# Eight sums over partitions moved from TensorE to GpSimd in a one-core decoder layer

## Chip, cores and metric

The kernel runs on one core of one Trainium2 chip. The metric is the device time of one execution in microseconds, lower is better.

## What is computed

One layer of a decoder trunk, 256 tokens of width 2048, all in float32:

```python
mod = silu(c) @ w_ada + b_ada                 # 6 x 2048: sh1, sc1, gt1, sh2, sc2, gt2
h = rmsnorm(x, g_pre_mix) * (1 + sc1) + sh1
y = token_mixer(h)                            # 4 GLA heads, 8 attention heads, merged by two sigmoid gates
x = x + gt1 * rmsnorm(y, g_post_mix)
h = rmsnorm(x, g_pre_ffn) * (1 + sc2) + sh2
y = conv_ffn(h)                               # up to 2 x 5632, causal conv of width 3, gelu gate, down
out = x + gt2 * rmsnorm(y, g_post_ffn)
```

In the mixer, one input projection gives the GLA and attention operands and the two gates; each branch is projected to 2048, `merged = sigmoid(gate_a) * y_a + sigmoid(gate_b) * y_b`, and a projection `w_o` follows.

## The kernel before

**Weights.** Every weight passes through four buffers `raw`, `hi`, `lo` of 128x2048 (fill number `w`, buffer `w % 4`). SyncE loads fill `w` into `raw` in two transfers once TensorE has finished fill `w - 4` (semaphore `used`). ScalarE rounds it to `hi` (`split_hi`), VectorE makes the remainder `lo = raw - hi` (`split_lo`, L761), and TensorE multiplies activations, themselves split in two, by `hi` and by `lo` (`tokens_still`, `weights_still`, `one_row_tile`; all their products have line L1246). ScalarE and VectorE work three fills ahead (`split_lo(w + 3)`).

**Stages**, one after the other on TensorE: the gate stage (32 fills, and one for the low-rank factor), four heads of 12 fills (`HEAD_N`; tile `n` of head `I`), the merge stage (`MERGE`: 16 fills `m`, four column blocks `cb` of 512 with two branches and two halves each), the output projection with `w_o` (16 fills `kt`), the up projection (22 passes of four fills) and the down projection (44 fills). Every engine's order is written out by hand as loops over these numbers; nothing is scheduled at run time.

**In a head**, VectorE makes per tile the decay operands `Mb` of a level and selects into `A` (L924 to L934), for which TensorE's `gram` products wait, in tile 9 the softmax, and in the last tile of head 3 the first two remainders of the branch outputs `og_om` (`branch_lo`, L960), which the merge stage needs.

**In the merge stage**, VectorE multiplies and adds a block's two branches (`merged(cb)`, L1030 to L1033, at m = 5, 7, 11, 15), TensorE transposes the result (`merged_T`, L1475, one tile later), and VectorE makes its remainder (`merged_lo`, L1038).

**Modulation.** `silu(c) @ w_ada` is made without TensorE's weights: a *unit* is one row block of `w_ada`, 128 partitions x 1024 columns, which VectorE scales by a column of `silu(c)` and adds to an accumulator. Sixteen units make a *part*, 1024 columns of `mod` as 128 partial sums. The parts of `sh1` and `sc1` belong to the gate stage and are left alone by the change. The other eight (0 to 3: `sh2` and `sc2`; 4, 5: `gt1`; 6, 7: `gt2`) alternate between `acc_a` and `acc_b`, from part 6 on in `acc_a` alone. GpSimd issues their transfers (L440) into two buffers `ada`, each when the unit before last has been used (`ada_used`), and behind them on the same queue the bias rows (L415) and the post-norm gains G1 and G2 (L428, L435). VectorE's `ada_unit` stands behind the split, `UNITS_H[n]` times in a head's tile, `UNITS_L[n]` in the last head's, `UNITS_M[m]` in the merge stage's; in the up projection `row_unit` (L1170) does two per pass.

**The sums over the 128 partitions** are TensorE's. For parts 0 to 3, at tile 5 of head 0 to 3, eight products with the accumulator as weights and a column of ones give the part as columns, which VectorE copies into `mods` (L1017). For parts 4 to 7, `row_sums` multiplies the accumulator by an all-ones matrix: two products of 128x512, four records, whose every row is the sum; VectorE multiplies them into the gain (`gate_row`, L1062). Two stand in the output projection (kt = 0 and 2), one each in passes 8 and 17 of the up projection. `zero_acc` clears an accumulator for parts 4 to 7, and a bias row is loaded into it.

## Time and profile before

| | us |
|---|---|
| median of 3 runs | 1479.89 |
| lowest, highest | 1479.24, 1482.47 |
| the profiled execution's own time | 1481.32 |
| its span, first to last instruction | 1479.5 |
| TensorE busy in it | 1444.7 |
| VectorE busy in it | 1103.2 |
| mean granted clock of TensorE | 0.997 |

In the profile PE is TensorE's matmul, PEld its weight load, DVE is VectorE, ACT ScalarE, POOL GpSimd, SP SyncE. Times are from the span's start. A timeline row gives start, duration, engine, line, operation, output and inputs, shape and count, and in brackets the engine's idle time ahead of it and what ended that. Durations of pipelined matmuls are modelled, so their spacing is read from the starts.

### The profile page before, as it was taken

What the parts mean: (1) busy time and instruction counts of PE and PEld (TensorE: products, weight loads), DVE (VectorE), ACT (ScalarE), POOL (GpSimd) and SP (SyncE); (2) the same over time, 40 slices, a digit from 0 to 9 for tenths busy, and PEclk for the clock granted to TensorE, in tenths of its full rate; (3) what the DMA queues carried; (4) which work ended last, traced back from release to release, by engine and by line L of the source; (5) the groups of instructions that cost most, each with busy time, mean ns of one, the idle gap of its engine ahead of it and who ended that gap; (6) DMA issues with size and microseconds to landing.
All of it is one profiled execution on the core that took longest, in us unless ns stands there. A gap on an engine that the chain in (4) does not pass through costs nothing.

```text
span 1479.5 us, 19948 instructions
## 1 busy us (share of the span) xinstructions
PE 1444.7 (98%) x7444; PEld 1230.8 (83%) x7444; DVE 1103.2 (75%) x1129; ACT 701.6 (47%) x711; POOL 86.5 (6%) x177
## 2 busy tenths in 40 slices
PE   4999999999999999999999999999999999999998
PEld 2878888888888888878888888888888888888886
DVE  6999988898888988855687877777776666555445
ACT  4454444354535465424565455545544545434443
POOL 3000001111111000100000000000000000000000
PEclk9999999999999999999999999999999999999999
DMA  9999879898979877866467777677765555555553
GB/s 362 386 387 379 292 252 323 263 296 272 313 245 317 266 243 260 303 239 218 163 223 235 239 231 237 202 224 238 242 228 182 187 194 188 189 195 198 191 190 129
DMA packets 235816, 367.07 MB, mean 248 GB/s; under 512 B 11487, under 2 KB 161505, under 8 KB 234994
## 3 DMA queue, kind: packets, MB, share of 16 engines
q1 hardware_dynamic: 215824, 294.69, 59.5%
q0 software_dynamic: 18848, 69.23, 13.6%
q10 hardware_dynamic: 1090, 2.40, 0.4%
q8 instruction: 37, 0.61, 0.2%
q14 instruction: 17, 0.14, 0.0%
HBM read 364.18 MB, written 2.10 MB: 248 GB/s over the span
## 4 chain that ended last, share of the span: by engine, by line
PE 86%; DMA 6%; DVE 5%; ACT 1%; issue 1%; SPq 0%; DVEq 0%
PE ps L1246 85%; DMA ada<-in_w_ada 4%; DMA raw<-in_w_in 1%; DVE acc_a L790 1%; DVE acc L771 1%; DMA adar<-in_w_ada 1%; DVE lo L761 1%; ACT hi L454 1%; DMA raw<-in_w_o 0%; ACT yt L672 0%; PE ps L1475 0%; DVE acc_b L790 0%; SPq L312 0%; DVE yo L1094 0%; PE ps L1406 0%
## 5 line engine op out<-in xcount | busy, mean ns | idle before, releaser
L1246 PE MATMUL ps<-hT,hi 128*128 128x512 f32 x1936 | 466.0, 393 | 0.9 <-DVE hT L1116 0.9
L1246 PEld LDWEIGHTS ps<-hT,hi 128*128 128x128 f32 x1936 | 356.2, 188 | 72.3 <-issue 2.0
L454 ACT ACTIVATE hi<-raw 128x2048 fp32r<-128x2048 f32 x116 | 222.1, 1916 | 280.6 <-DMA raw<-in_w_in 185.5
L761 DVE TENSOR_TENSOR lo<-raw,hi 128x2048 fp32r<-128x2048 f32 x117 | 266.9, 2285 | 63.1 <-ACT hi L454 62.9
L1246 PEld LDWEIGHTS ps<-hT,lo 128*128 128x128 f32 x1936 | 248.2, 191 | 9.4
L1246 PE MATMUL ps<-hT,lo 128*128 128x256 f32 x1936 | 251.1, 283 | 0.0
L1201 DVE TENSOR_TENSOR lo<-raw,hi 128x2048 fp32r<-128x2048 f32 x88 | 199.1, 2290 | 32.6 <-ACT hi L719 32.4
L1246 PE MATMUL ps<-hi,hT 128*128 128x512 f32 x768 | 185.4, 394 | 1.1 <-DVE hT L815 0.9
L1246 PE MATMUL ps<-hi,asp 128*128 128x512 f32 x704 | 175.9, 389 | 0.0
L719 ACT ACTIVATE hi<-raw 128x2048 fp32r<-128x2048 f32 x88 | 165.6, 1906 | 11.2 <-DMA raw<-in_w_up 9.3
L1246 PEld LDWEIGHTS ps<-hi,hT 128*128 128x128 f32 x768 | 143.1, 189 | 32.5 <-issue 2.9
L1246 PEld LDWEIGHTS ps<-hi,asp 128*128 128x128 f32 x704 | 132.1, 188 | 27.5
L1225 DVE TENSOR_TENSOR lo<-raw,hi 128x2048 fp32r<-128x2048 f32 x40 | 91.7, 2292 | 49.5 <-ACT hi L732 49.5
L440 POOL DMA_DIRECT2D ada<-in_w_ada x128 | 68.1, 532 | 879.4 <-DVE acc_a L1170 295.2
L1246 PE MATMUL ps<-lo,asp 128*128 128x512 f32 x352 | 96.1, 389 | 0.0
L1246 PE MATMUL ps<-lo,hT 128*128 128x512 f32 x384 | 94.8, 389 | 0.0
L697 ACT ACTIVATE cv<-ps 128x512 f32<-128x512 f32 x44 | 26.4, 600 | 134.3 <-PE ps L1246 134.3
L771 DVE SCALAR_TENSOR_TENSOR acc<-adar,scol,acc 128x1024 f32<-128x1024 f32 x60 | 77.0, 1284 | 10.8 <-DMA adar<-in_w_ada 6.7
L1246 PEld LDWEIGHTS ps<-lo,hT 128*128 128x128 f32 x384 | 72.1, 188 | 15.0
L1246 PEld LDWEIGHTS ps<-lo,asp 128*128 128x128 f32 x352 | 66.0, 188 | 13.8 <-DVE lo L761 0.2
L708 ACT ACTIVATE asp<-aT 128x256 fp32r (+1 forms) x44 | 18.0, 416 | 124.7 <-PE ps L1246 124.7
L732 ACT ACTIVATE hi<-raw 128x2048 fp32r<-128x2048 f32 x40 | 76.0, 1901 | 0.0
(207 smaller groups left out, 1269.6 us busy)
## 6 DMA issues: line engine op xcount, KB each, us to landing
raw<-in_w_up SPq DMA_DIRECT2D x176, 512.0 KB, 4.4
raw<-in_w_in SPq DMA_DIRECT2D x162, 512.0 KB, 5.7
ada<-in_w_ada POOLq DMA_DIRECT2D x128, 512.0 KB, 4.9
raw<-in_w_down SPq DMA_DIRECT2D x88, 512.0 KB, 4.2
adar<-in_w_ada SPq DMA_DIRECT2D x64, 512.0 KB, 10.3
raw<-in_w_o SPq DMA_DIRECT2D x32, 512.0 KB, 5.1
raw<-in_w_gla_out SPq DMA_DIRECT2D x16, 512.0 KB, 5.1
raw<-in_w_moba_out SPq DMA_DIRECT2D x16, 512.0 KB, 5.3
```

What stands on the lines that cost most here:

```text
L440: pool.dma_start(ada[:, u % 2, :], wada[:, t, PART_COL[part]:PART_COL[part] + 1024]).then_inc(ada_in[u % 2], 16)
L454: act.activation(hi[:, w % 4, :], raw[:, w % 4, :], ACT.Copy).then_inc(hi_done, 1)
L697: act.activation(cv[:, :, :], ps[:, 2 * g:2 * g + 2, TOK:], ACT.Copy).then_inc(cross5, 1)
L708: act.activation(asp[:, k, 0:TOK], aT[:, ds(kt, 1), :], ACT.Copy).then_inc(a_hi, 1)
L719: act.activation(hi[:, w % 4, :], raw[:, w % 4, :], ACT.Copy).then_inc(hi_done, 1)
L732: act.activation(hi[:, (w + 3) % 4, :], raw[:, (w + 3) % 4, :], ACT.Copy).then_inc(hi_done, 1)
L761: dve.tensor_tensor(lo[:, w % 4, :], raw[:, w % 4, :], hi[:, w % 4, :].bitcast(F32), ALU.subtract).then_inc(lo_done, 1)
L771: ins = dve.scalar_tensor_tensor(a, adar[:, u % 8, :], scol[:, t:t + 1], a, ALU.mult, ALU.add)
L790: ins = dve.scalar_tensor_tensor(acc[:, :], ada[:, u % 2, :], scol[:, t:t + 1], acc[:, :], ALU.mult, ALU.add)
L1201: dve.tensor_tensor(lo[:, k, :], raw[:, k, :], hi[:, k, :].bitcast(F32), ALU.subtract).then_inc(lo_done, 1)
L1225: dve.tensor_tensor(lo[:, k, :], raw[:, k, :], hi[:, k, :].bitcast(F32), ALU.subtract).then_inc(lo_done, 1)
L1246: return pe.matmul(out_, lhsT, rhs, start=start, stop=stop)
```

## The change

All eight sums are made by GpSimd: `partition_all_reduce` over the accumulator, in place, every partition gets the sum. It stands on GpSimd's queue ahead of the third unit transfer of the next part, and one on a single column is made ahead of all. For parts 0 to 3 a row goes to DRAM (`part_rows`) and comes back as columns three units later; `acc_zero` and the first unit of parts 2 and 3 wait for that. `gate_row` reads the accumulator itself. G1 is loaded at unit 68 instead of 90, and x in the merge stage (behind fill 8) instead of the output projection. The units are dealt out anew: 54 in the heads instead of 67 (with the gate stage's 12 as before), 19 in the merge stage instead of 17, 11 in the output projection instead of none; where a tile has two, one stands ahead of the split. TensorE's queue has lost its sums, in the output projection the transposes of block 3 stand behind the third half tile, and in the up projection each sum's gate row moves from pass 8 to 9 and 17 to 19.

```diff
@@ -73,10 +73,13 @@
     UNITS_3 = {25: 1, 26: 1, 27: 1, 28: 2, 29: 2, 30: 2, 31: 2, 32: 1}
-    UNITS_H = [2, 1, 1, 1, 1, 1, 1, 2, 2, 2, 2, 2]
-    UNITS_L = [2, 1, 1, 1, 1, 1, 1, 2, 2, 1, 0, 0]
-    UNITS_M = [1] * 13 + [2] + [1] * 2
-    assert sum(UNITS_3.values()) + (HEADS - 1) * sum(UNITS_H) + sum(UNITS_L) + sum(UNITS_M) == 6 * KT
+    UNITS_H = [[1, 1, 1, 1, 1, 1, 0, 1, 2, 1, 2, 1],
+               [1, 1, 1, 2, 1, 1, 1, 1, 0, 1, 2, 1],
+               [1, 1, 1, 2, 1, 2, 1, 1, 1, 1, 0, 1],
+               [1, 1, 2, 1, 2, 1, 2, 1, 1, 1, 1, 1]]
+    UNITS_M = [0, 1, 2, 1, 2, 1, 2, 2, 2, 1, 1, 1, 0, 1, 2, 0]
+    UNITS_O = [1] * 11 + [0] * 2
+    assert sum(UNITS_3.values()) + sum(sum(h) for h in UNITS_H) + sum(UNITS_M) + sum(UNITS_O) == 6 * KT
...
@@ -336,13 +341,13 @@
                 load_grid(W_MERGE + m, wmo if branch else wgo, 4 * half, 4, 512 * cb, 512)
+                if m == 8:
+                    sp.wait_ge(oo_ready, 4)
+                    sp.dma_start(x2[:, :, :], x_v).then_inc(xr_in, 16)
             for kt in range(KT):
                 sp.wait_ge(used, W_WO + kt - 3)
                 load_row(W_WO + kt, wo, kt)
-                if kt == 4:
-                    sp.wait_ge(oo_ready, 4)
-                    sp.dma_start(x2[:, :, :], x_v).then_inc(xr_in, 16)
             def load_up(i, w, n):
...
@@ -415,14 +420,33 @@
                 pool.dma_start(acc[0:1, :], b_ada[:, PART_COL[part]:PART_COL[part] + 1024]).then_inc(bias_in, 16)
+            def sum_rows(part, acc):
+                pool.wait_ge(ada_used, KT * part + KT)
+                pool.partition_all_reduce(acc[:, :], acc[:, :], P, bass.bass_isa.ReduceOp.add).then_inc(row_sum, 1)
+                if part < 4:
+                    pool.wait_ge(row_sum, part + 1)
+                    pool.dma_start(part_rows[part:part + 1, :], acc[0:1, :]).then_inc(row_out, 16)
+
+            def row_columns(part):
+                pool.wait_ge(row_out, 16 * (part + 1))
+                pool.dma_start(modsf[:, M_SH2 * KT + 8 * part:M_SH2 * KT + 8 * part + 8],
+                               part_rows[part].rearrange("(k p) -> p k", p=P), allow_slow_non_contiguous=True).then_inc(part_in, 16)
+
+            made(pool.memset(stat[:, 9:10], 0.0))
+            made(pool.partition_all_reduce(stat[:, 9:10], stat[:, 9:10], P, bass.bass_isa.ReduceOp.add))
+
             pool.wait_ge(mod_done, 4)
             for u in range(8 * KT):
                 part, t = divmod(u, KT)
+                if t == 2 and part:
+                    sum_rows(part - 1, acc_b if part in (2, 4, 6) else acc_a)
+                if t == 5 and 0 < part < 5:
+                    row_columns(part - 1)
                 if u == 4 * KT - 2:
                     bias_row(4, acc_a)
                 if u == 5 * KT - 2:
                     bias_row(5, acc_b)
-                if u == 6 * KT - 6:
+                if u == 4 * KT + 4:
                     pool.wait_ge(pv_done, HEADS)
...
@@ -438,6 +462,7 @@
                 pool.dma_start(ada[:, u % 2, :], wada[:, t, PART_COL[part]:PART_COL[part] + 1024]).then_inc(ada_in[u % 2], 16)
+            sum_rows(7, acc_a)
         @block.scalar
...
@@ -791,6 +816,10 @@
             def zero_acc(part):
+                if part < 6:
+                    dve.wait_ge(part_in, 16 * (part - 1))
+                else:
+                    dve.wait_ge(g_ready, part - 5 if part == 6 else 3)
                 dve.memset((acc_b if part == 5 else acc_a)[:, :], 0.0).then_inc(acc_zero, 1)
...
@@ -1012,15 +1041,12 @@
                         tail(I - 1, n)
-                    if n == 6:
-                        dve.wait_ge(mod_done, 4 + I + 1)
-                        dve.tensor_copy(modsf[:, M_SH2 * KT + 8 * I:M_SH2 * KT + 8 * I + 8], ps[:, 6, 0:8]).then_inc(part_read, 1)
-                    if (I, n) == (2, 8):
+                    if (I, n) == (3, 4):
                         zero_acc(4)
-                    if (I, n) == (3, 7):
-                        zero_acc(5)
+                    if UNITS_H[I][n] > 1:
+                        ada_unit()
                     split_lo(w + 3)
-                    for k in range(UNITS_H[n] if I < HEADS - 1 else UNITS_L[n]):
+                    if UNITS_H[I][n]:
                         ada_unit()
...
@@ -1050,31 +1076,39 @@
                     merged({5: 0, 7: 1, 11: 2, 15: 3}[m])
+                if m == 6:
+                    zero_acc(5)
+                if UNITS_M[m] > 1:
+                    ada_unit()
                 split_lo(w + 3)
-                for k in range(UNITS_M[m]):
+                if UNITS_M[m]:
                     ada_unit()
-            assert ada_count[0] == 6 * KT
-
-            def gate_row(k, G, bank, sem_in):
+
+            def gate_row(k, G, acc, sem_in):
                 cs = slice(1024 * (k % 2), 1024 * (k % 2 + 1))
-                dve.wait_ge(g_done, k + 1)
+                dve.wait_ge(row_sum, 4 + k + 1)
                 dve.wait_ge(sem_in, 16)
-                dve.tensor_tensor(G[:, cs], ps[:, bank:bank + 2, :].rearrange("p b n -> p (b n)"), G[:, cs], ALU.mult).then_inc(g_ready, 1)
+                dve.tensor_tensor(G[:, cs], acc[:, :], G[:, cs], ALU.mult).then_inc(g_ready, 1)
             for kt in range(KT - 3):
-                if kt == 0:
-                    gate_row(0, G1, 4, g1_in)
                 split_lo(W_WO + kt + 3)
                 if kt == 0:
                     merged_lo(3)
-                    gate_row(1, G1, 4, g1_in)
-                if kt == 2:
+                if UNITS_O[kt]:
+                    ada_unit()
+                if kt == 3:
+                    gate_row(0, G1, acc_a, g1_in)
+                if kt == 4:
                     zero_acc(6)
-                if kt == 4:
+                if kt == 8:
+                    dve.wait_ge(part_in, 64)
                     link(dve.tensor_tensor(mods[:, M_SH2:M_GT2, :], mods[:, M_SH2:M_GT2, :],
                                            cols[:, M_SH2 * KT:5 * KT].rearrange("p (m k) -> p m k", m=2), ALU.add))
                     dve.scalar_tensor_tensor(mods[:, M_SC2, :], mods[:, M_SC2, :], 1.0, cols[:, COL_PRE2:COL_PRE2 + KT],
                                              ALU.add, ALU.mult).then_inc(mods_ready, 1)
+
+            assert ada_count[0] == 6 * KT
+            gate_row(1, G1, acc_b, g1_in)
             def y_sum(branch, tt):
...
@@ -1202,18 +1236,20 @@
                     if sums is not None and n == 2:
-                        gate_row(sums - 4, G2, 4 if sums == 6 else 6, g2_in)
+                        gate_row(sums - 4, G2, acc_a, g2_in)
                         if sums == 6:
                             zero_acc(7)
             up_pass(0, row=(6, 0), tasks=(2, 3))
             with dve.Fori(1, 8) as i:
                 up_pass(i, row=(6, 0))
-            up_pass(8, sums=6)
-            with dve.Fori(9, 17) as i:
-                up_pass(i, row=(7, 9))
-            up_pass(17, sums=7)
-            with dve.Fori(18, UP_ITERS - 1) as i:
+            up_pass(8)
+            up_pass(9, sums=6)
+            with dve.Fori(10, 18) as i:
+                up_pass(i, row=(7, 10))
+            up_pass(18)
+            up_pass(19, sums=7)
+            with dve.Fori(20, UP_ITERS - 1) as i:
                 up_pass(i)
...
@@ -1443,17 +1479,10 @@
                         gram(I, n - 3)
-                    if n == 5:
+                    if n == 9:
+                        pe.wait_ge(evac, 5 * I + 4)
                         if I:
                             pe.wait_ge(om_f, I)
-                        pe.wait_ge(ada_used, KT * I + KT)
-                        acc = acc_b if I % 2 else acc_a
-                        for j in range(8):
-                            ins = mm(ps[:, 6, j:j + 1], acc[:, P * j:P * (j + 1)], ones[:, 0:1])
-                        ins.then_inc(mod_done, 1)
-                    if n == 9:
-                        pe.wait_ge(evac, 5 * I + 4)
-                        pe.wait_ge(part_read, I + 1)
                         for hd in range(2):
...
@@ -1516,22 +1540,15 @@
                     one_row_tile(k, mT[:, kt, :], kt == 0, False, 0, W_WO + kt + 1)
-                if kt == 0:
-                    pe.wait_ge(ada_used, 5 * KT)
+                if kt == 2:
+                    merged_T(3)
                     pe.wait_ge(gated_y, 7)
-                    row_sums(acc_a, 4)
-                if kt == 1:
-                    merged_T(3)
-                if kt == 2:
-                    pe.wait_ge(ada_used, 6 * KT)
-                    pe.wait_ge(g_ready, 1)
-                    row_sums(acc_b, 4)
+                    one_row_tile(W_WO % 4, mT[:, 0, :], True, False, 1, W_WO + 1, (0, 1))
+                    one_row_tile((W_WO + 1) % 4, mT[:, 1, :], False, False, 1, W_WO + 2, (0, 1))
                     pe.wait_ge(mt_ready, 4)
-                    one_row_tile(W_WO % 4, mT[:, 0, :], True, False, 1, W_WO + 1, (2, 3))
-                    pe.wait_ge(g_ready, 2)
-                    one_row_tile(W_WO % 4, mT[:, 0, :], True, False, 1, W_WO + 1, (0, 1)).then_inc(used, 1)
-                    for j in (1, 2):
-                        one_row_tile((W_WO + j) % 4, mT[:, j, :], False, False, 1, W_WO + j + 1).then_inc(used, 1)
+                    one_row_tile(W_WO % 4, mT[:, 0, :], True, False, 1, W_WO + 1, (2, 3)).then_inc(used, 1)
+                    one_row_tile((W_WO + 1) % 4, mT[:, 1, :], False, False, 1, W_WO + 2, (2, 3)).then_inc(used, 1)
+                    one_row_tile((W_WO + 2) % 4, mT[:, 2, :], False, False, 1, W_WO + 3).then_inc(used, 1)
                 if 3 <= kt < KT - 4:
...
@@ -1572,18 +1589,9 @@
                                   None if order == range(4) else h2_is_ready).then_inc(used, 1)
-                    if sums is not None and n == 1:
-                        pe.wait_ge(ada_used, KT * sums + KT)
-                        row_sums(acc_a, 4 if sums == 6 else 6)
             up_pass(0, order=UP_FIRST)
-            with pe.Fori(1, 8) as i:
-                up_pass(i)
-            up_pass(8, 6)
-            with pe.Fori(9, 17) as i:
-                up_pass(i)
-            up_pass(17, 7)
-            with pe.Fori(18, UP_ITERS) as i:
+            with pe.Fori(1, UP_ITERS) as i:
                 up_pass(i)
```

The places the prediction speaks of follow as the instructions stand on an engine.

GpSimd, end of part 4 (`G_113` is G1, `acc_a` holds part 4, `acc_b` parts 3 and 5). Before, from unit 62 on:

```order
L415 DMA acc_a<-in_b_ada 1x16x64
L440 DMA ada<-in_w_ada 128x1024 x16
L415 DMA acc_b<-in_b_ada 1x16x64
L440 DMA ada<-in_w_ada 128x1024 x12
L428 DMA G_113<-in_g_post_mix 128x2048
```

Now:

```order
L420 DMA acc_a<-in_b_ada 1x16x64
L464 DMA ada<-in_w_ada 128x1024 x4
L425 ISA acc_b<-acc_b 128x1024
L428 DMA part_rows<-acc_b 16x1x64
L464 DMA ada<-in_w_ada 128x1024 x2
L452 DMA G_113<-in_g_post_mix 128x2048
L464 DMA ada<-in_w_ada 128x1024
L432 DMA mods<-part_rows 128x8x1
L464 DMA ada<-in_w_ada 128x1024 x9
```

The sum (`ISA`) and the row's transfer stand between two unit transfers, the gain's load two units behind them.

VectorE, merge stage, from block 0's sum at m = 5 to block 1's at m = 7 (`lo<-raw,hi` is a split, `acc` with `ada` a unit, `GA` the block). Before:

```order
L1033 TENSOR_TENSOR GA<-GA 128x2x512
L761 TENSOR_TENSOR lo<-raw,hi 128x2048
L790 SCALAR_TENSOR_TENSOR acc_b<-ada,scol,acc_b 128x1024
L761 TENSOR_TENSOR lo<-raw,hi 128x2048
L790 SCALAR_TENSOR_TENSOR acc_b<-ada,scol,acc_b 128x1024
L1038 TENSOR_TENSOR mT<-ps,mT 128x4x256
L1030 TENSOR_TENSOR GA<-GA,ps 128x2x512
```

Now:

```order
L1059 TENSOR_TENSOR GA<-GA 128x2x512
L786 TENSOR_TENSOR lo<-raw,hi 128x2048
L815 SCALAR_TENSOR_TENSOR acc_a<-ada,scol,acc_a 128x1024
L823 MEMSET acc_b 128x1024
L815 SCALAR_TENSOR_TENSOR acc_a<-ada,scol,acc_a 128x1024
L786 TENSOR_TENSOR lo<-raw,hi 128x2048
L815 SCALAR_TENSOR_TENSOR acc_a<-ada,scol,acc_a 128x1024
L1064 TENSOR_TENSOR mT<-ps,mT 128x4x256
L1056 TENSOR_TENSOR GA<-GA,ps 128x2x512
```

A memset and a unit have come between the two blocks.

TensorE, start of the output projection. Before:

```order
L1246 MATMUL ps<-lo,mT 128x512 x4
L1246 MATMUL ps<-acc_a,ones 128x512 x2
L1246 MATMUL ps<-hi,mT 128x512 x8
L1246 MATMUL ps<-lo,mT 128x512 x4
L1475 MATMUL ps<-ident,GA 128x128 x8
L1246 MATMUL ps<-hi,mT 128x512 x8
L1246 MATMUL ps<-lo,mT 128x512 x4
L1246 MATMUL ps<-acc_b,ones 128x512 x2
```

Now:

```order
L1282 MATMUL ps<-lo,mT 128x512 x4
L1282 MATMUL ps<-hi,mT 128x512 x8
L1282 MATMUL ps<-lo,mT 128x512 x4
L1282 MATMUL ps<-hi,mT 128x512 x8
L1282 MATMUL ps<-lo,mT 128x512 x4
L1504 MATMUL ps<-ident,GA 128x128 x8
```

The sums are gone, and the transposes of block 3 come one half tile later.

## Rows read from the trace of the kernel before

**Rows 1.** The page, busy time and share of the span by engine.

```profile
PE 1444.7 (98%) x7444; PEld 1230.8 (83%) x7444; DVE 1103.2 (75%) x1129; ACT 701.6 (47%) x711; POOL 86.5 (6%) x177
```

**Rows 2.** TensorE's timeline, head 0 (start, us, engine, line, tiles, count).

```profile
266.51 1.84 PE L1246 MATMUL ps<-ones,acc_a 128*128 128x1 f32 x16
268.22 3.92 PE L1246 MATMUL ps<-hi,hT 128*128 128x512 f32 x16
...
273.79 0.60 PE L1246 MATMUL ps<-Mb 128*128 128x128 f32 x4
```

**Rows 3.** TensorE's timeline, start of the output projection (in brackets: idle before).

```profile
633.88 1.07 PE L1246 MATMUL ps<-lo,mT 128*128 128x512 f32 x4
636.94 3.65 PE L1246 MATMUL ps<-acc_a,ones 128*128 128x512 f32 x4 [1.99 <-DVE GA L1030]
639.68 2.77 PE L1246 MATMUL ps<-hi,mT 128*128 128x512 f32 x8
```

**Rows 4.** Busy time by stretch: five engines, then PEclk, DMA share, GB/s.

```profile
637.00:640.50 3.50, 3.50 (x5) 1.47 (x6) 3.46 (x3) 0.60 (x2) 0.00 (x0) 0.52 0.82 294
```

**Rows 5.** TensorE's timeline, up projection, pass 8.

```profile
928.66 1.88 PE L1246 MATMUL ps<-acc_a,ones 128*128 128x512 f32 x4
929.98 4.22 PE L1246 MATMUL ps<-hT,hi 128*128 128x512 f32 x16
```

**Rows 6.** GpSimd's timeline, making of the masks.

```profile
11.29 1.17 POOL L405 TENSOR_SCALAR_AFFINE_SELECT maskf<-maskf 128x128 f32<-128x128 f32 x1
```

**Rows 7.** VectorE's timeline, same stretch.

```profile
11.00 1.28 DVE L771 SCALAR_TENSOR_TENSOR acc<-adar,scol,acc 128x1024 f32<-128x1024 f32 x1 [5.20 <-DMA adar<-in_w_ada]
```

**Rows 8.** Timeline of all engines, start of the second sub-layer.

```profile
732.47 1.90 POOL L433 CAST hi<-raw 128x2048 fp32r<-128x2048 f32 x1 [61.01 <-DVE x L1094]
...
733.85 0.61 DVE L1100 TENSOR_SCALAR diag<-ident,stat 128x128 f32<-128x128 f32 x1
```

**Rows 9.** VectorE's timeline, head 0 and end of head 3.

```profile
262.80 0.28 DVE L924 TENSOR_TENSOR Mb<-qk,eb 128x128 f32<-128x128 f32 x1
...
537.98 2.34 DVE L960 TENSOR_TENSOR og_om<-oo,og_om 128x1024 fp32r<-128x1024 f32 x2
```

**Rows 10.** TensorE's timeline, merge stage and end of the output projection.

```profile
539.29 3.89 PE L1246 MATMUL ps<-hi,og_om 128*128 128x512 f32 x16
...
580.41 1.03 PE L1475 MATMUL ps<-ident,GA 128*128 128x128 f32 x8
...
592.21 1.04 PE L1475 MATMUL ps<-ident,GA 128*128 128x128 f32 x8
...
614.86 1.03 PE L1475 MATMUL ps<-ident,GA 128*128 128x128 f32 x8
...
713.30 1.07 PE L1246 MATMUL ps<-lo,mT 128*128 128x512 f32 x4
```

**Rows 11.** VectorE's timeline, same stretches.

```profile
573.12 2.29 DVE L761 TENSOR_TENSOR lo<-raw,hi 128x2048 fp32r<-128x2048 f32 x1 [4.94 <-ACT hi L454]
...
578.91 1.23 DVE L1033 TENSOR_TENSOR GA<-GA 128x1024 f32<-128x1024 f32 x1
...
590.36 1.23 DVE L1033 TENSOR_TENSOR GA<-GA 128x1024 f32<-128x1024 f32 x1
...
607.42 2.29 DVE L761 TENSOR_TENSOR lo<-raw,hi 128x2048 fp32r<-128x2048 f32 x1 [2.36 <-ACT hi L454]
...
613.21 1.22 DVE L1033 TENSOR_TENSOR GA<-GA 128x1024 f32<-128x1024 f32 x1
...
708.03 2.29 DVE L761 TENSOR_TENSOR lo<-raw,hi 128x2048 fp32r<-128x2048 f32 x1 [2.47 <-ACT hi L454]
```

**Rows 12.** The page's DMA issues: count, KB each, us to landing.

```profile
ada<-in_w_ada POOLq DMA_DIRECT2D x128, 512.0 KB, 4.9
```

**Rows 13.** Instructions on tile acc_a (ns min/median/max, first and last start).

```profile
L794 DVE MEMSET acc_a<- x3: 912/912/912, 443.8 to 939.7; 128x1024 f32 x3
```

**Rows 14.** Busy time by stretch, up projection: length, then PE, PEld, DVE, ACT, POOL.

```profile
739.00:1242.00 503.00, 502.80 (x2865) 442.15 (x2866) 379.86 (x389) 264.04 (x265) 16.99 (x32) 1.00 0.67 219
```

17 lines of the change are left out of this document (6 added, 11 removed).

## The prediction

> **What bounds the kernel now.** I read four views in turn. The page's busy shares: TensorE works in 1444.7 of the 1479.5 us of the span [rows 1], so nearly every microsecond taken out of its queue is gained, and every one it waits is lost. TensorE's timeline: where the eight sums stand in its queue and what they cost [rows 2 to 4]. The timelines of VectorE and GpSimd: how close VectorE runs to what TensorE needs, and what the two do to each other [rows 6 to 11]. Last the transfers behind the modulation units, which GpSimd issues and which now stand behind its sums [rows 12].
>
> **What leaves TensorE.** A column sum of a head (eight products of width 1, 16 records) starts at 266.51 and the next weights' product at 268.22 [rows 2]: 1.7 us, four times, 6.8 us. The first gate row sum: the third product group of the output projection's first tile starts at 633.88 and its four records take 0.9, so the queue would go on at 634.8; it goes on at 639.68 [rows 3]. In these 4.9 us lie 1.99 us of waiting for the last merge product (VectorE) and four records at a granted clock of 0.52, that is mostly at 1.2 GHz, right after that idle time [rows 3, 4]; the eight products behind it take 2.77 instead of some 2.0. Together 5.6 us, and the idle time need not come back, since the wait for that merge product moves behind three half tiles (8 us). The second row sum and the two of the up projection are four records at full clock: 929.98 - 928.66 = 1.3 and some 0.4 on the group behind, 4.22 for 16 products against 3.9 [rows 5, 2], so 1.7 each, 5.1 us. Sum: 6.8 + 5.6 + 5.1 = **17.5 us less**. Nothing hides this work in the kernel before, and it was all on the path.
>
> **What is added.** *A sum on GpSimd, 128x1024, eight times.* No row shows one. One pass over 1024 columns on GpSimd costs 0.95 us (half of the 1.90 of its cast [rows 8]): the lower end. Adding 128 partitions one after another at that rate is 122 us: the upper end. A tree over 128 partitions has seven steps and one to hand the result back, eight passes: 7.6 us. I take **8 us** as the estimate, nearest to what a pass costs.
>
> [...]
>
> *Where a hold H costs.* At the last head's tile 9 the sum of part 3 starts. Behind it VectorE has to do the select, the softmax scale, a split, now a unit too (1.28 [rows 7]), and the first remainder of the branch outputs, which before was ready at 539.15 for a product that started at 539.29 [rows 9, 10]. VectorE gains about the unit that tile 8 no longer has, so the slack stays about 0.4: H - 0.4. The sum of part 4 starts behind merge tile 9; block 2's merge ends at 614.43 and TensorE wants it at 614.86 [rows 10, 11]. The idle 2.36 us ahead of the split at 607.42 will be eaten by the denser units, so the price is H. The sum of part 5 starts some 1.1 us ahead of the split at 708.03; that takes 2.29 and its lo tile is used at 713.30, so 713.3 - 706.9 - 2.3 = 4.1 us are free [rows 10, 11]. The sums of parts 0 to 2 start behind a tile of a head, the first at about 262. The decay operands that VectorE makes next, at 262.80, are used at 273.79 (1.7 earlier without the column sum) [rows 9, 2], so some 9 us are free there, and as much in the others. In the up projection VectorE is idle for a quarter (379.86 of 503 [rows 14]), so two more are free up to about 5.5. With H = 2: 1.6 + 2 = **3.6 us**.
>
> *The denser merge stage.* Before, each merge tile has one unit, and the merges of blocks 0 and 1 are done 0.3 and 0.6 us before TensorE's transposes (580.14 for 580.41; 591.59 for 592.21) [rows 10, 11]. Now the load of the post-mix gain (1 MB) stands on GpSimd's queue ahead of the second unit of tile 2, and waits for the last attention product, which TensorE makes behind that tile. The unit's transfer shares the bandwidth with that load: VectorE loses some 4 us there (an estimate), and can get them back from the 4.94 of idle time in tile 4 [rows 11], where a second unit now stands too. Two units in a tile also need two transfers, each 4.9 us from its issue [rows 12], which waits for the unit before last. I work the first merge out as 1.8 to 3 us late. Tile 6 adds a memset (0.91 [rows 13]) and a unit ahead of block 1's merge: 2.2 against the 0.6, at least 1.6 more, with late transfers 3. Between 1.6 and 8 in all (the upper end with the lower clock again after a 2 us stall, as in [rows 4]) I take **6 us**.
>
> *The rest.* Loading x, 2 MB, in the merge stage puts it beside tiles whose lo is some 10 us ahead; it makes unit transfers later, which is in the 6. It leaves the output projection, where it did not make TensorE wait: 0. Four row transfers and four column transfers from GpSimd are 0.5 us each to issue; the latter are 1024 pieces of 4 bytes, no row shows such a one. Even at 4 us each they delay one unit transfer, and lo tiles are ahead by more: 0, at most 2 each. VectorE's waits for them (two first units, the memsets) come 11 or more units after the sum starts: 0; behind such a wait would stand splits. The small first sum and what it loads run ahead of GpSimd's wait for the gate stage, and VectorE's wait for the masks is met before them: 0. Gate rows from SBUF instead of PSUM: 1.2 us either way. The eleven units in the output projection stand behind splits that wait for their weights (2.5 us of idle time at 708.03 [rows 11]): 0.
>
> **The sum.** The profiled execution took 1481.32 us: -17.5 + 3.6 + 6 = -7.9, so 1473.4. The median of the runs is 1.4 lower, **1472.0**. If nothing of the costs comes, 1481.3 - 17.5 - 1.4 = 1462.
>
> **Rivals.** *A: the forecast*, faster by 5 to 17 us, 1462 to 1475. Chance 0.52.
>
> *B: VectorE is held for the whole sum, and it lasts 8 us or more.* Place: the four exposed sums. Price: (X - 0.4) + X + (X - 4.1) + 2 (X - 5.5), with X = 8: 7.6 + 8 + 3.9 + 5 = 24.5, with the merge's 6 and -17.5: +13, 1493. With X = 10: 1504. It decides from X = 5.3, where the costs meet the 17.5. For it speak rows 6 to 8; against it, that those are instructions that stream all the time. Chance 0.33.
>
> *C: held, but X near 5*: 9.6 + 0.9 + 6 - 17.5 = -1, so 1479. Chance 0.13.
>
> *D: the sum is serial over partitions*, 122 us. Two units are loaded ahead, then VectorE and TensorE wait: some 105 us for each of the six sums before the up projection and some 90 for the two in it, +800 us, about 2290. The Trainium skill, "GPSIMD Engine Reference", section "Cross-partition — where GPSIMD wins", gives 247.7 us for a reduction over partitions at 128x2048, half of which is close to that; no run so far shows it. Against it: one mask select of GpSimd over all partitions takes a few tenths of a microsecond, so partitions are not its unit of work [rows 6]. Chance 0.02.
>
> **The numbers.** A measurement of this kernel tells 0.2% (3 us) from no change. Faster 0.52 (A), same 0.13 (C), slower 0.35 (B and D). The likeliest case gives 1472; its own range is 1462 to 1475. The range of 8 in 10 reaches down to 1461 and up through C and B to X = 10: 1504. What is left out is B with a longer sum and D.
>
> **What would show it.** No products with width 1 from the heads on and no all-ones products on acc_a or acc_b: TensorE's busy time down by some 14 us. The sums' spacing on GpSimd near 8 us, from the sum to the row's transfer behind it. Units and splits that start in a sum: if they run on with 2.3 and 1.3 us, A holds; if they end with the sum, B or C. TensorE waiting for the merge sum in tiles 6 and 8, some 2 to 3 us each, and for og_om at merge tile 0 by H. The clock at full speed at the start of the output projection. I am wrong if the merge stage shows no wait (then nearer 1466), if VectorE waits for unit transfers in the heads, or if a sum takes over 10 us.

## The result, and the profile after the change

The changed kernel takes **1490.54 us** (median of 6 runs, 1488.53 to 1493.25) against 1479.57 of the kernel before (6 runs, 1477.43 to 1483.11): ratio 1.0077, interval 1.0066 to 1.0089, slower by 0.8%. The forecast was 1472.0, range 1461 to 1504. The profiled execution took 1491.12 us, its span 1489.4.

First, the page of the profile after: TensorE's busy time is down by 7.8 us [rows 1] where some 14 were forecast, and the span is 9.9 longer, so TensorE now waits, and part of its work runs at half clock (below).

```profile
PE 1436.9 (96%) x7364; PEld 1225.8 (82%) x7364; DVE 1129.7 (76%) x1125; ACT 702.6 (47%) x711; POOL 151.4 (10%) x195
```

GpSimd's groups by line (instruction count, then busy us and mean ns, then idle time before): a sum takes 6.06 to 6.11 us, once 7.33. The estimate was 8.

```profile
L425 POOL PARTITION_ALL_REDUCE acc_a<-acc_a x5 | 31.6, 6328 | 21.4 <-DVE acc_a L1204 21.3
L425 POOL PARTITION_ALL_REDUCE acc_b<-acc_b x3 | 18.2, 6069 | 0.1
```

**VectorE in a sum.** Timelines of GpSimd and VectorE after the change, at the sums of parts 3, 4 and 5:

```profile
524.58 6.08 POOL L425 PARTITION_ALL_REDUCE acc_b<-acc_b  x1
...
617.48 7.33 POOL L425 PARTITION_ALL_REDUCE acc_a<-acc_a  x1
...
718.47 6.06 POOL L425 PARTITION_ALL_REDUCE acc_b<-acc_b  x1
```

```profile
524.64 6.24 DVE L1040 TENSOR_SCALAR ssb<-ssb,stat 128x128 f32<-128x128 f32 x4
...
619.76 4.55 DVE L815 SCALAR_TENSOR_TENSOR acc_b<-ada,scol,acc_b 128x1024 f32<-128x1024 f32 x1 [0.93 <-DMA ada<-in_w_ada]
...
718.49 8.81 DVE L786 TENSOR_TENSOR lo<-raw,hi 128x2048 fp32r<-128x2048 f32 x2 [0.87 <-ACT hi L479]
```

The four scalings took 1.05 us before, a unit takes 1.28, two splits take 4.5. VectorE loses 5.2, 3.3 and 4.3 us here. So the hold is most of the sum, not two passes of it (2 us).

The rows say where in the sum VectorE is let go, if a held instruction is taken to need its normal length from then on. These are the first and the third scaling one by one, and the split ahead of the sum of part 4:

```profile
524.64 4.51 DVE L1040 TENSOR_SCALAR ssb<-ssb,stat 128x128 f32<-128x128 f32 x1
...
529.33 1.41 DVE L1040 TENSOR_SCALAR ssb<-ssb,stat 128x128 f32<-128x128 f32 x1
...
616.55 2.28 DVE L786 TENSOR_TENSOR lo<-raw,hi 128x2048 fp32r<-128x2048 f32 x1
```

The first scaling (normally 0.28) is let go at 528.9, the first of the two splits (718.49, 6.61 long for 2.29) at 722.8: both 4.3 us after the start of their sum. The sum of part 4 started in the middle of a split; counted from that split's end (618.83) it took 6.0 us and let the unit go at 623.03, 4.2 us in. The scalings were held a second time: the third took 1.41 us and ended at 530.74, where the sum ends too (530.66).

**TensorE's waits.** Its timeline after, at the first merge product, the transposes of the first and third merge, and tile 12 of the output projection:

```profile
535.50 6.46 PE L1282 MATMUL ps<-hi,og_om 128*128 128x512 f32 x16 [4.47 <-issue]
...
585.91 1.97 PE L1504 MATMUL ps<-ident,GA 128*128 128x128 f32 x8 [6.32 <-DVE GA L1059]
...
627.89 1.33 PE L1504 MATMUL ps<-ident,GA 128*128 128x128 f32 x5 [5.48 <-DVE GA L1059]
...
725.15 1.96 PE L1282 MATMUL ps<-lo,mT 128*128 128x512 f32 x4 [1.99 <-DVE lo L786]
```

The first wait is put down to "issue", but VectorE's timeline shows what the products wait for. The first remainder of `og_om` stands behind the held scalings and ends just ahead of 535.50 (two records, 2.35 us in all):

```profile
534.19 2.35 DVE L989 TENSOR_TENSOR og_om<-oo,og_om 128x1024 fp32r<-128x1024 f32 x2
```

The windows at the ends of these waits (length, busy time of PE, PEld, DVE, ACT and POOL, then PEclk, DMA share, GB/s): each of the waits of 4.5 to 6.3 us ends at half the clock, 1.2 instead of 2.4 GHz, for some 6.8 us, of which the first part is idle anyway. The 16 products at 535.50 take 6.46 us for 3.9. Behind the 2 us wait at 725 it is 3.4 us.

```profile
534.16:541.00 6.84, 5.50 (x13) 4.36 (x14) 6.84 (x7) 1.91 (x1) 0.72 (x2) 0.50 0.26 86
581.95:588.80 6.85, 2.89 (x11) 2.70 (x12) 6.82 (x6) 3.46 (x3) 0.53 (x1) 0.50 0.97 362
626.32:633.20 6.88, 5.31 (x17) 4.54 (x18) 6.85 (x5) 4.66 (x3) 1.08 (x2) 0.50 0.47 149
725.31:728.72 3.41, 3.41 (x9) 2.63 (x10) 3.12 (x2) 0.00 (x0) 0.00 (x0) 0.50 0.03 6
```

The wait at 585.91 has no sum near it. VectorE's timeline ahead of it:

```profile
565.94 1.28 DVE L815 SCALAR_TENSOR_TENSOR acc_a<-ada,scol,acc_a 128x1024 f32<-128x1024 f32 x1 [3.98 <-DMA ada<-in_w_ada]
...
581.05 1.28 DVE L815 SCALAR_TENSOR_TENSOR acc_a<-ada,scol,acc_a 128x1024 f32<-128x1024 f32 x1 [5.13 <-DMA ada<-in_w_ada]
582.25 1.21 DVE L1056 TENSOR_TENSOR GA<-GA,ps 128x1024 f32<-128x1024 f32 x1
```

VectorE stands 5.13 us for a unit's transfer, and the merge is queued behind that unit. The transfers of 560 to 586 (issues, KB each, median us to landing): 7.6 us for a unit, where the same stretch before has 4.4 and the whole of that kernel 4.9 [rows 12], beside x's 2 MB in 12 us, with every DMA engine busy (share 1.02 after, 0.82 in the same stretch before).

```profile
ada<-in_w_ada POOLq DMA_DIRECT2D x5, 512.0 KB, 7.6
...
x<-in_x SPq DMA_DIRECT2D x1, 2048.0 KB, 12.0
```

**Where the time went.** From the starts in TensorE's timeline I cut each profiled execution into stretches: the first weights' product, the gram product of head 0, the first merge product, the transposes of merges 0, 1 and 2, the output projection, the up projection, the down projection, the end. All in us. They are single executions, whose total differs from the kernel's median by up to 5 us (those of quarters, 1479.68, and of up_sums, 1474.14, were the fastest of their kernels); totals are compared by medians and ratios, the table tells places.

```
                    start  head 0   heads  merge  T0-T1  T1-T2   T2-O  output     up   down
before              37.65  214.68  286.96  41.12  11.79  22.65  17.21  107.14 493.51 246.78
after               39.22  213.86  282.43  50.40  13.60  28.38  19.78  105.14 490.05 246.51
no_sums             38.92  213.84  277.69  47.93  13.88  24.55  17.30  103.97 490.03 246.75
no_sums_loads_late  39.74  213.48  277.69  44.60  13.60  24.73  17.28  107.63 490.03 246.51
no_sums_even        39.32  213.79  277.69  41.32  13.69  26.21  18.93  107.49 490.06 246.94
x_merge             37.86  214.13  287.33  41.14  16.68  26.40  18.91  104.45 493.51 247.25
quarters            39.47  213.73  280.72  49.32  13.60  25.47  17.28  101.77 490.07 246.52
up_sums             39.92  213.46  285.26  41.14  11.77  22.69  17.21  104.05 490.04 246.84
```

The change gains 4.5 us in the heads, 2.0 in the output projection and 3.5 in the up projection, and loses 19.4 in the four stretches of the merge stage and 0.7 ahead of the gram product. The output projection's column is firm to some 3 us only: up_sums leaves everything up to its end as in the kernel before, and took 104.05 there for 107.14. The other rows are the experiments below.

### The profile page after: what moved, and what is told of

It reads as the page before. It is cut to its first block, busy times and chain, and to the rows that moved or that the text cites. A ratio compares the mean times of both kernels' runs of the same rounds, so it can differ in the third digit from the quotient of the medians.

```text
span 1489.4 us, 19738 instructions
## 1 busy us (share of the span) xinstructions
PE 1436.9 (96%) x7364; PEld 1225.8 (82%) x7364; DVE 1129.7 (76%) x1125; ACT 702.6 (47%) x711; POOL 151.4 (10%) x195
## 4 chain that ended last, share of the span: by engine, by line
PE 87%; DMA 5%; DVE 4%; issue 2%; ACT 1%; SPq 0%; DVEq 0%; POOL 0%
PE ps L1282 87%; DMA ada<-in_w_ada 2%; DMA raw<-in_w_o 1%; DVE lo L786 1%; DVE acc L796 1%; DMA adar<-in_w_ada 1%; DMA raw<-in_w_in 1%; DVE acc_a L815 1%; ACT hi L479 1%; DVE GA L1056 0%; DVE GA L1057 0%; ACT yt L697 0%; PE ps L1442 0%; DVE mT L1064 0%; SPq L317 0%
## 5 line engine op out<-in xcount | busy, mean ns | idle before, releaser
L479 ACT ACTIVATE hi<-raw 128x2048 fp32r<-128x2048 f32 x116 | 222.2, 1917 | 286.3 <-DMA raw<-in_w_in 176.5
L786 DVE TENSOR_TENSOR lo<-raw,hi 128x2048 fp32r<-128x2048 f32 x117 | 274.9, 2353 | 51.2 <-ACT hi L479 50.9
L1235 DVE TENSOR_TENSOR lo<-raw,hi 128x2048 fp32r<-128x2048 f32 x88 | 198.8, 2290 | 31.1 <-ACT hi L744 31.0
L744 ACT ACTIVATE hi<-raw 128x2048 fp32r<-128x2048 f32 x88 | 165.3, 1905 | 7.6 <-DMA raw<-in_w_up 6.8
L1261 DVE TENSOR_TENSOR lo<-raw,hi 128x2048 fp32r<-128x2048 f32 x40 | 91.7, 2292 | 49.6 <-ACT hi L757 49.6
L1221 DVE SCALAR_TENSOR_TENSOR cv<-up,cols,cv 128x256 f32<-128x256 f32 x88 | 46.7, 532 | 39.1 <-ACT cv L726 38.7
```

The costliest lines, as they stand in the source:

```text
L479: act.activation(hi[:, w % 4, :], raw[:, w % 4, :], ACT.Copy).then_inc(hi_done, 1)
L744: act.activation(hi[:, w % 4, :], raw[:, w % 4, :], ACT.Copy).then_inc(hi_done, 1)
L786: dve.tensor_tensor(lo[:, w % 4, :], raw[:, w % 4, :], hi[:, w % 4, :].bitcast(F32), ALU.subtract).then_inc(lo_done, 1)
L1221: dve.scalar_tensor_tensor(cv[:, ct, :], up[:, ct, 1:TOK + 1], cols[:, ds(f + COL_CONV + 2 * FT, 1)], cv[:, ct, :], ALU.mult, ALU.add).the ...
L1235: dve.tensor_tensor(lo[:, k, :], raw[:, k, :], hi[:, k, :].bitcast(F32), ALU.subtract).then_inc(lo_done, 1)
L1261: dve.tensor_tensor(lo[:, k, :], raw[:, k, :], hi[:, k, :].bitcast(F32), ALU.subtract).then_inc(lo_done, 1)
```

## The experiments

Theory 1: the sums of parts 3 to 5 hold VectorE where TensorE waits for it. Theory 2: the loss is the loads' and the denser units'. A ratio is to the kernel before. The difference between two changed kernels is taken from their ratios; where their medians tell something else, both stand.

**Cut the sums to one column.** In no_sums all eight, in no_sums_3_5 those of parts 3 to 5; the other 1023 columns are left unsummed, everything else stays.

```diff
-                pool.partition_all_reduce(acc[:, :], acc[:, :], P, bass.bass_isa.ReduceOp.add).then_inc(row_sum, 1)
+                pool.partition_all_reduce(acc[:, 0:1], acc[:, 0:1], P, bass.bass_isa.ReduceOp.add).then_inc(row_sum, 1)
```

> The changed kernel with every one of the eight sums of 1024 columns cut to its first column (a sum of 128x1, which leaves the modulation's second half wrong); transfers, waits, units and the small first sum stay. What is left over the kernel before is the price of all else. Theory 'three sums (parts 3 to 5) hold VectorE where TensorE needs it': their stalls and the low clock behind them go, 1490.5 - 14 to - 18, some 1473 to 1476. Rival 'units, x and transfers of the merge stage cost the 10 us': 1486 or more.

> The changed kernel with the sums of parts 3, 4 and 5 alone cut to their first column, those of parts 0 to 2, 6 and 7 whole. Theory: the five that stay cost nothing, so the same time as with all eight cut, within 2 us (1473 to 1477). Rival 'each sum costs': 5 x 2 to 6 us above it, 1485 or more.

Measured: no_sums 1476.80 us, ratio 0.9983 (0.9969 to 0.9996); no_sums_3_5 1478.93, 0.9991 (0.9978 to 1.0005). Against the changed kernel's 1.0077 the eight sums cost 0.94% = 13.9 us, and parts 3 to 5 make 12.7 of them. The five sums that stay cost 1.2 (2.1 by medians), inside the uncertainty. Theory 1 holds for the sums. TensorE is busy for 1431.3 us in no_sums, 13.4 less than before, near the 14 forecast. But if 17.5 us have left TensorE's path, as forecast, and without any sum only 2.5 are gained, then 15 us are lost to something else. In TensorE's timeline of no_sums the wait ahead of the first merge's transposes is still there:

```profile
578.38 0.90 PE L1504 MATMUL ps<-ident,GA 128*128 128x128 f32 x3 [5.86 <-DVE GA L1059]
```

**A sum again.** Sums already made are made a second time. The edit of extra_merge; in extra_heads the condition is t == 8 for parts 1 and 2.

```diff
+                if (part, t) in ((4, 8), (5, 3)):
+                    again = acc_b if part in (2, 4, 6) else acc_a
+                    pool.wait_ge(row_sum, part)
+                    made(pool.partition_all_reduce(again[:, :], again[:, :], P, bass.bass_isa.ReduceOp.add))
```

> The changed kernel (1490.5 us) with the sum of part 3 made a second time behind unit 71 (merge tile 4, ahead of the first merge) and that of part 4 behind unit 82 (right behind the first time, merge tiles 9 to 12). Wrong values in the scale row and the first half of the gate row. Theory 'VectorE is held for the whole of a sum' (6.1 us each, nothing free in the merge stage): 2 x 6.1 = +12 us, 1502, a little more where TensorE's clock drops once more. Rival 'VectorE loses only the two passes, and the stalls of the merge stage are its transfers and denser units': at most 2 x 2 = +4 us, 1494 to 1495.

> The changed kernel (1490.5 us) with the sums of parts 0 and 1 made a second time behind units 23 and 39, in tiles of heads 0/1 and 1/2. Wrong values in the shift row. If the place decides (VectorE some 9 us ahead of what TensorE needs in a head): 0 to +2 us, 1490 to 1493. If a sum costs TensorE something wherever it stands (bandwidth of SBUF or of the transfers, the issue of the weight transfers behind it): 2 x 6 = +12, 1502, as in the merge stage.

Measured: extra_heads 1489.33, ratio 1.0059 (1.0040 to 1.0078), nothing lost for two more sums. extra_merge 1495.37, 1.0094 (1.0070 to 1.0119): 2.5 us for two by the ratios, 4.8 by the medians, and 5.5 by the two profiled spans, so some 5 us, far below theory 1's 12 and at the rival's upper end. TensorE's and VectorE's timelines of extra_merge say why:

```profile
585.51 1.75 PE L1508 MATMUL ps<-ident,GA 128*128 128x128 f32 x7 [5.86 <-DVE GA L1063]
...
632.69 1.54 PE L1508 MATMUL ps<-ident,GA 128*128 128x128 f32 x6 [10.22 <-DVE GA L1063]
```

```profile
574.16 4.07 DVE L819 SCALAR_TENSOR_TENSOR acc_a<-ada,scol,acc_a 128x1024 f32<-128x1024 f32 x1 [2.35 <-DMA ada<-in_w_ada]
...
580.65 1.28 DVE L819 SCALAR_TENSOR_TENSOR acc_a<-ada,scol,acc_a 128x1024 f32<-128x1024 f32 x1 [0.22 <-DMA ada<-in_w_ada]
```

The one at 572.67 lay in time in which VectorE stands for unit transfers anyway (the wait for the next unit falls from 5.13 to 0.22) and cost nothing; the one at 627.07 made a wait of 10.22 out of 5.48. So the total met the rival's number for another reason than the rival's: each hold is long (the unit at 574.16 takes 4.07 for 1.28), but a hold costs only what VectorE has no other wait for.

**Sums in quarters.**

```diff
-                pool.partition_all_reduce(acc[:, :], acc[:, :], P, bass.bass_isa.ReduceOp.add).then_inc(row_sum, 1)
+                for j in range(4):
+                    cs = slice(256 * j, 256 * (j + 1))
+                    ins = pool.partition_all_reduce(acc[:, cs], acc[:, cs], P, bass.bass_isa.ReduceOp.add)
+                ins.then_inc(row_sum, 1)
```

> The changed kernel with each sum made as four sums of 256 columns one after another (all results right). Some 1.8 us each, 7.3 in all. Theory 'an instruction of GpSimd holds VectorE from its first to its last access': VectorE gets its turn between two quarters, the sum stretches over VectorE's work, and TensorE waits 2 to 4 us less at each of the three places: 1480 to 1486. Rival 'GpSimd keeps the port over the whole group': 3 x 1.2 more, 1492 to 1496.

Measured: 1484.50 us, ratio 1.0034 (1.0020 to 1.0049): 6 us less than the changed kernel, as the theory had it. GpSimd's, then VectorE's timeline at the sum of part 3:

```profile
524.69 8.76 POOL L427 PARTITION_ALL_REDUCE acc_b<-acc_b  x4
```

```profile
524.73 1.93 DVE L1043 TENSOR_SCALAR ssb<-ssb,stat 128x128 f32<-128x128 f32 x4
526.59 3.17 DVE L789 TENSOR_TENSOR lo<-raw,hi 128x2048 fp32r<-128x2048 f32 x1
529.68 2.11 DVE L818 SCALAR_TENSOR_TENSOR acc_a<-ada,scol,acc_a 128x1024 f32<-128x1024 f32 x1
531.71 3.25 DVE L992 TENSOR_TENSOR og_om<-oo,og_om 128x1024 fp32r<-128x1024 f32 x2
```

The two engines take turns: each group of VectorE loses 0.8 to 0.9 us to one quarter (3.5 in all), the sum stretches to 8.76, and TensorE waits 2.79 us for the first merge product instead of 4.47.

**The loads.** x back in the output projection (x_late), the post-mix gain back ahead of unit 90 (g1_late), both (x_g1_late), and both with the sums cut (no_sums_loads_late).

```diff
-                if m == 8:
-                    sp.wait_ge(oo_ready, 4)
-                    sp.dma_start(x2[:, :, :], x_v).then_inc(xr_in, 16)
...
+                if kt == 4:
+                    sp.wait_ge(oo_ready, 4)
+                    sp.dma_start(x2[:, :, :], x_v).then_inc(xr_in, 16)
...
-                if u == 4 * KT + 4:
+                if u == 6 * KT - 6:
```

> The changed kernel with x loaded in the output projection's tile 4 and the post-mix gain ahead of unit 90, as before the change; the sums and units stay. Theory: of the stall ahead of the first merge's transposes (6.3 us idle, then 6.8 us at half clock) the two unit transfers that take 9 us beside x are the larger part, so -5 to -8 us: 1482 to 1486. Rival 'all of the loss is the held VectorE and its denser units': within 1 us of 1490.5.

> The changed kernel with x loaded in the output projection's tile 4 again, the post-mix gain's load left where the change put it. Moving both back gave 1490.4 (no gain), the gain alone 1489.2. Theory 'x only moves the wait': 2 to 4 us less ahead of the first merge, as much more in the output projection: 1489 to 1492. Rival 'x costs in the merge stage and nothing in the output projection': 1485 to 1487.

> The changed kernel with the load of the post-mix gain alone back ahead of unit 90; x stays in the merge stage. With both moved back the wait ahead of the first merge was 2.5 us instead of 6.7, and 3 us of new waits for weights came in the output projection. Theory: x beside the output projection's weights made the latter, and the gain's load a part of the former: 1486 to 1489. Rival 'x is what delays the unit transfers, the gain does nothing': 1490 to 1492.

> The changed kernel with all eight sums cut to one column and x and the gain's load moved back as well. Left of the change: the units' new distribution, the row and column transfers, the order of the output projection, the small first sum. With the sums cut alone the stretch from the first merge product to the first merge's transposes took 47.9 us (41.1 before). Theory 'the two loads hold the units' transfers up there': 41 to 44 us now, and the output projection 2 to 6 us longer: 1473 to 1477. Rival 'the units' new distribution alone does it': 46 to 48 us there, 1477 or more.

Measured: x_late 1486.92, ratio 1.0054 (1.0040 to 1.0069), 3.4 us less; g1_late 1489.16, 1.0063 (1.0041 to 1.0084), 2.1 less (1.4 by medians); both 1490.35, 1.0058 (1.0037 to 1.0079), 2.8 less by the ratios and 0.2 by the medians, not 5.5; with the sums cut 1476.99, 0.9975 (0.9962 to 0.9987), 1.2 less than with the loads early. The table shows where, with the sums cut: the merge stretch falls from 47.9 to 44.6, and the output projection rises from 104.0 to 107.6 (in g1_late, with x still in the merge stage, it takes 107.5 too, so x alone does not explain that). In x_late the first merge's transposes wait 1.95 us instead of 6.32:

```profile
581.59 1.09 PE L1504 MATMUL ps<-ident,GA 128*128 128x128 f32 x8 [1.95 <-DVE GA L1059]
```

In g1_late they wait 1.36 us, and those of the second merge 4.44. Either load moved away takes most of the first wait, and part of it comes back further on. Of x alone I expected too little (the rival's 1485 to 1487 was right), and of both too much: the median is where the rival had it.

**x in the merge stage of the kernel before**, nothing else changed.

> The kernel before with x loaded behind merge weight 8, as in the change, and nothing else. Its units stand one in each tile. Theory 'x delays the unit transfers, and VectorE has 0.3 us to spare at the first merge': 3 to 6 us more ahead of the first merge's transposes, 0 to 2 less in the output projection: 1482 to 1485. Rival 'it is hidden without the second units': within 1 us of the kernel before.

Measured: 1487.06 us, ratio 1.0051 (1.0033 to 1.0068): 7.5 us. The size was above my theory's and the place was another: not the first merge but the second, and less so the third. ScalarE's, VectorE's and TensorE's timelines of x_merge:

```profile
587.00 1.92 ACT L454 ACTIVATE hi<-raw 128x2048 fp32r<-128x2048 f32 x1 [7.76 <-DMA raw<-in_w_gla_out]
```

```profile
588.95 2.29 DVE L761 TENSOR_TENSOR lo<-raw,hi 128x2048 fp32r<-128x2048 f32 x1 [5.85 <-ACT hi L454]
```

```profile
597.14 1.18 PE L1475 MATMUL ps<-ident,GA 128*128 128x128 f32 x5 [4.75 <-DVE GA L1033]
```

It is the weights that come late: the half fill issued at 575.6 lands at 587.0, 11.4 us, where the four issued from 564 on ahead of x took 5.1 to 7.1. The split that waits for them stands ahead of the merge in VectorE's queue, as the unit does after the change.

**x in four pieces**, with the sums in quarters.

```diff
-                if m == 8:
+                if m in (8, 10, 12, 14):
                     sp.wait_ge(oo_ready, 4)
-                    sp.dma_start(x2[:, :, :], x_v).then_inc(xr_in, 16)
+                    sp.dma_start(x2[:, :, 256 * (m - 8):256 * (m - 6)], x_v[:, :, 256 * (m - 8):256 * (m - 6)]).then_inc(xr_in, 16)
```

> The changed kernel with each sum in four quarters and x loaded in four pieces of 512 columns behind merge weights 8, 10, 12 and 14. Quarters alone: 1484.5. Theory 'the 2 MB in one piece delay two unit transfers to 9 us ahead of the first merge': 3 to 5 us less there and nothing more later: 1479 to 1481. Rival 'the pieces delay as much in sum': 1483 to 1486.

Measured: 1482.02, ratio 1.0018 (1.0003 to 1.0034), 2.4 us less than in quarters alone, between the theory (1479 to 1481) and the rival (1483 to 1486). It is the fastest of the kernels with all eight sums on GpSimd, and still not faster than the kernel before.

**The units' spread.** As no_sums_loads_late, with five units ahead of the first merge, one in a tile.

```diff
-    UNITS_M = [0, 1, 2, 1, 2, 1, 2, 2, 2, 1, 1, 1, 0, 1, 2, 0]
+    UNITS_M = [1, 1, 1, 1, 1, 1, 2, 2, 2, 2, 1, 1, 0, 1, 2, 0]
```

> As no_sums_loads_late (sums cut to one column, both loads late: 1477.0), with the merge stage's nineteen units spread as 1 1 1 1 1 1 2 2 2 2 1 1 0 1 2 0 instead of 0 1 2 1 2 1 2 2 2 1 1 1 0 1 2 0: five units ahead of the first merge sum, as in the kernel before, not six, and no two in a tile. Theory 'two units in a tile wait for their transfers, and the sixth delays the first merge': the 3.7 us ahead of the first merge's transposes go to under 1, 1473 to 1475. Rival 'it is the heads' lateness that stays': 1476 to 1478.

Measured: 1477.64, ratio 0.9993 (0.9984 to 1.0002), no gain: 0.7 us more by the medians, 2.7 by the ratios. TensorE's timeline at the transposes of merges 0, 1 and 2:

```profile
572.12 1.04 PE L1504 MATMUL ps<-ident,GA 128*128 128x128 f32 x8
...
585.81 0.44 PE L1504 MATMUL ps<-ident,GA 128*128 128x128 f32 x2 [1.76 <-DVE GA L1059]
...
612.02 1.24 PE L1504 MATMUL ps<-ident,GA 128*128 128x128 f32 x5 [3.33 <-DVE GA L1059]
```

The wait ahead of the first merge is gone (41.3 us, 41.1 before the change), as the theory said, but comes back at the second and third. In no_sums_loads_late there was none ahead of the second, and 1.84 ahead of the third.

**Fewer sums on GpSimd.** All from the kernel before, with its units and loads. hybrid: parts 0 to 3, 6 and 7. hybrid2: parts 0 to 2, 6 and 7, those of 1 and 2 moved by 3 and 4 units. hybrid2_ns: the same without the small first sum. hybrid3: 0, 6 and 7. up_sums: 6 and 7, no small sum. small_only: the small sum and nothing else. The core of hybrid3:

```diff
+                if (part, t) in ((1, 2), (7, 2)):
+                    sum_rows(part - 1, acc_a)
+                if (part, t) == (1, 5):
+                    row_columns(part - 1)
...
-                    if n == 5:
+                    if I and n == 5:
```

> The kernel before, its units, loads of x and of the gain unchanged, with six of the eight sums on GpSimd (parts 0 to 3 in the heads, 6 and 7 in the up projection, a small one first) and the two that would stand in the merge stage (parts 4 and 5) on TensorE as before. Theory: 6 x 1.7 = 10.2 us leave TensorE, the small first sum costs 1.3 at the start, the holds are free in these places: 1479.6 - 8.9 = 1471, up to 1474 if a head's sum sticks out by one or two us. Rival 'a sum costs wherever it stands': 1479.6 - 10.2 + 6 x 4 = 1493.

> The kernel before with five sums on GpSimd: parts 0 to 2 in the heads, those of parts 1 and 2 moved to tiles 5 and 4 of heads 1 and 2 (they stood just ahead of the gram product, where TensorE then waited 7.3 and 3.2 us), and parts 6 and 7 in the up projection; parts 3 to 5 stay on TensorE. Theory 'the place decides': 5 x 1.7 = 8.5 us less, 1.5 more at the start, 1479.6 - 7 = 1472.5, up to 1475. Rival 'with two units in each late tile of a head VectorE has no 6 us to spare anywhere': waits of 3 to 7 us in the heads stay, 1480 to 1490.

> The same without the small first sum. Theory: the start comes back (-1.5 us), and what the first sum loads stands ahead of the sum in head 0 instead, where it holds up unit transfers for some 6 to 12 us; two are loaded ahead, so VectorE's units wait but its splits behind them too: 1471 to 1477. If the load is paid in full there: 1479 or more.

> The kernel before with three sums on GpSimd: part 0's in head 0 (in hybrid2 at 261.3, where no wait followed until 409) and parts 6 and 7 in the up projection; the small first sum as in the change. Theory: 3 x 1.7 = 5.1 us less, 0 to 1 at the start: 1475 (1474 to 1477), at or below the kernel with the two of the up projection alone (1477.0). Rival 'a sum in a head with two units in each late tile comes back as a wait of 3 us in the next head': 1477 to 1480.

> The kernel before with only the two sums of the up projection (parts 6 and 7) on GpSimd, no small first sum, no row transfers, all else as before. In every kernel with these two on GpSimd the up projection took 490.05 us instead of 493.51. Theory: 3.5 us less, 1476 (ratio 0.9977). If what the first sum loads holds unit transfers up there (6.5 us of GpSimd ahead of it): 0 to 3 us back, 1476 to 1479.

> The kernel before plus the small first sum (128x1) and nothing else of the change. Theory: it makes GpSimd wait for some 10 us ahead of its first mask select, the masks come 20 us later, and the first weights' product starts 1.5 us later (39.2 instead of 37.7 in the changed kernel): 1481. Rival 'it costs nothing, the start is late by other things': within 0.5 us of the kernel before.

Measured, with the ratio to the kernel before: hybrid 1490.68, 1.0066 (1.0044 to 1.0087); hybrid2 1486.21, 1.0037 (1.0019 to 1.0055); hybrid2_ns 1486.91, 1.0044 (1.0024 to 1.0063); hybrid3 1480.03, 0.9998 (0.9982 to 1.0013); up_sums 1477.03, 0.9985 (0.9970 to 1.0000); small_only 1480.07, 1.0006 (0.9993 to 1.0019).

My theory failed for all that have a sum in a head: with the old units a sum there is not free. GpSimd's, VectorE's and TensorE's timelines of hybrid, at the sum of part 1:

```profile
326.46 6.06 POOL L421 PARTITION_ALL_REDUCE acc_b<-acc_b  x1
```

```profile
326.19 1.74 DVE L972 RECIPROCAL rs<-rs 128x256 f32<-128x256 f32 x1
327.85 3.64 DVE L973 SCALAR_TENSOR_TENSOR tg<-tg,grt 128x512 f32<-128x512 f32 x1
331.41 0.68 DVE L976 TENSOR_TENSOR ot<-ot,rs 128x512 f32<-128x512 f32 x1
```

```profile
336.54 0.79 PE L1277 MATMUL ps<-Mb 128*128 128x128 f32 x2 [7.02 <-DVE Mb L950]
```

The hold falls just ahead of the decay products' operands, but it is only 3.0 us of these 7.0. The rest is lateness that was there before it. hybrid3, which has no sum at this place, shows it by itself: its only head sum (257.06) has no wait near it, and 76 us later TensorE waits in the next head. TensorE's, then VectorE's timeline:

```profile
333.09 0.59 PE L1277 MATMUL ps<-Mb 128*128 128x128 f32 x2 [3.68 <-DVE Mb L948]
```

```profile
323.89 1.28 DVE L811 SCALAR_TENSOR_TENSOR acc_b<-ada,scol,acc_b 128x1024 f32<-128x1024 f32 x1 [1.98 <-DMA ada<-in_w_ada]
```

VectorE isn't working all the way from the sum to that wait. It stands five times for a unit's transfer, 9.5 us in all, the last time right ahead of the operands. GpSimd, which issues these transfers, issued none from 256.50 to 265.65, while it made the sum and sent the row. So the lateness is handed on by the units' transfers. How much of it began as VectorE's hold and how much as a transfer issued late no run separates. The executions of hybrid3 fall in two groups, five from 1473.9 to 1476.1 us and seven from 1479.5 to 1483.7, and the trace is of the upper one.

So with the old units there were no 9 us in hand. The changed kernel has them: it does 13 units less ahead of the merge stage (66 instead of 79), and they come back in the merge stage and the output projection. That the units alone make the room is the likely reading and not shown: no run had the old units with all else of the change. The two sums in the up projection are a gain: 490.04 us instead of 493.51, at once as expected, and 1477.03 in all, 0.15% less than before, just at the edge of what can be told. It is the only full kernel here that I would put in place of the one before; the evidence for it is weak in the total and strong in the stretch, which took 490.03 to 490.07 us in every profiled kernel without TensorE's two sums and 493.51 in every one with them.

The small sum: in small_only GpSimd's first mask select starts at 13.03 instead of 1.67 us, and the first weights' product 1.9 us later, yet no loss can be told in the total. And the small sum's place isn't the reason: in up_sums, which has none and its first sum at 923, the select starts as late. So leaving it out could not bring the start back, as I had expected of hybrid2_ns. GpSimd's timelines of small_only and of up_sums:

```profile
13.03 1.11 POOL L386 TENSOR_SCALAR_AFFINE_SELECT ident<-ident 128x128 f32<-128x128 f32 x1 [11.61 <-issue]
```

```profile
13.05 1.10 POOL L386 TENSOR_SCALAR_AFFINE_SELECT ident<-ident 128x128 f32<-128x128 f32 x1 [11.63 <-issue]
```

## Why the prediction was wrong, point by point

- **What leaves TensorE, 17.5 forecast: right for the two sums that were tested alone.** The up projection gained 3.5 us for 3.4 forecast, and TensorE's busy time fell by 13.4 for 14 once the sums were cut (no_sums). The heads gained 9.3 there for 6.8, but they have 13 units less too. The output projection gained 3.2 for 7.3. Other waits came there (3.1 us in no_sums, all for `hi` or `lo` of a weight tile), and the 5.6 us of the first row sum were partly the luck of one execution: 1.99 of waiting and the low clock behind it. In up_sums, which keeps that sum on TensorE, the wait is 0.58 us and the clock stays up:

```profile
634.90 1.96 PE L1263 MATMUL ps<-acc_a,ones 128*128 128x512 f32 x4 [0.58 <-DVE GA L1039]
```

- **The length of a sum: 8 us estimated, 6.1 measured.** Right in size, a little long. A serial sum (rival D, 122 us) is out; that it is a tree is not shown.
- **Where a hold is free: right for the change, for the wrong reason.** No wait followed the sums of parts 0 to 2 and 6 and 7, as forecast. But I had read the 9 us of room in a head off the kernel before; the hybrids show that it isn't there with its units, or is used up by the late transfers of units.
- **The denser merge stage: the second step that failed, 6 us forecast.** Without any sum the four merge stretches take 10.9 us more than before (7.4 with the loads late too), and the output projection falls 4.1 short of its 7.3: together the 15 us that are left over in the total, where 6 were forecast. Moved loads, moved units: each run that took one cause away moved the waits on, and the total stayed within 1 us by medians (1476.8, 1477.0, 1477.6) and 3 by ratios. VectorE has 19 units there instead of 17 and 11 more in the output projection, and its merges are in the path. I costed those eleven units at 0 on 2.5 us of idle time in one tile, and 3.1 us of waits came there. What share is the units' own work and what their transfers' is open.
- **x "is in the 6", and 0 for what leaves the output projection.** In the kernel before, x in the merge stage costs 7.5 us by itself. I had looked at the units' transfers and held the weights to be 10 us ahead, while one then took 11.4 us. x stands on the weights' own queue, but the units' transfers on GpSimd's queue got slower as well (5.9 us in the median, 4.4 before), so whether the queue or the shared bandwidth did it is open.
- **The clock.** I had seen a drop of it behind a wait [rows 4] and given it only to the upper end of the merge term. It came with each of the three long waits, some 6.8 us long.
- **The small first sum at 0:** right in the total (1.0006, 0.9993 to 1.0019), though the masks came 20 us later and the first product 1.9.
- **Two readings.** The upper end of the range adds up to 1503 with X = 10, not 1504. And the few tenths of a microsecond for a mask select are not what [rows 6] shows, which is one of 1.17 us beside a working VectorE; the shortest in the same timeline take 0.29 to 0.41.

## What to carry to other kernels

A cross-partition sum on GpSimd is not free because GpSimd is idle: here it held VectorE's two-input instructions for the first 4.3 of its 6.06 us, so put it where VectorE itself has time in hand, not where TensorE has, or cut it in quarters. If the same engine issues transfers, count the time in which it issues none. Work taken from one stretch of an engine that is nearly full reappears in the next: room has to be counted for the schedule as it will be, with what was moved. A large load put beside a just-in-time stream delays that stream: here 2 MB that took 12.5 us made one of its transfers 4 to 6 us longer, and TensorE waited 4.75 us further on.

## What the runs showed of the chip

- A sum of 128x1024 over all partitions on GpSimd takes 6.06 us. One of 128x1 takes 0.33 to 0.5 in most places (0.46 after) and up to 2.95 in others (small_only). Four of 256 columns take 7.1 in the up projection and 8.6 to 10.0 with VectorE's turns between them (quarters).
- A two-input instruction of VectorE that meets such a sum goes on 4.2 to 4.4 us after the sum's start (six places in four kernels: after, hybrid, extra_heads, extra_merge).
- In a kernel that has such a sum anywhere, even in the up projection only, GpSimd stands 11.0 to 11.9 us ahead of its first mask select (0.23 in the kernel before). It stands again ahead of the first sum, 6.0 to 6.5 us for the small one, 6.7 for the first of hybrid2_ns and 8.7 for the first of up_sums.
- At the end of a TensorE wait of 4.5 to 6.3 us the granted clock was 0.50 for some 6.8 us in the changed kernel, behind one of 2 us in the output projection for 3.4. The length of the wait alone does not settle it: in extra_merge a wait of 5.12 us ahead of the first merge product had 3.4 us of it, and in g1_late a wait of 2.04 us (689.41) had none of it, the four products behind it taking 1.21 us.
- A 2 MB load took 12.0 us beside the weights' and the units' transfers, whose 0.5 MB then took 7.4 to 7.9 us in the median (4.4 to 5.9 in the same stretch before), with 381 GB/s in all (279 before). In x_merge it took 12.5, and one transfer of the weights 11.4.
